# Windowed attention with split fp32r values: no padded key blocks, residual read back in four transfers

## What is computed

```python
# 16 query heads, 4 key/value heads, head width 64, blocks of 128 tokens, window 128
kb, vb = bands(k), bands(v)            # for each block: previous, own and next block; zeros past the ends
scores = einsum('bnqhgd,bnkhd->bnhgqk', qb, kb) * 64 ** -0.5
scores = where(mask, scores, -1e30)    # |distance| <= 128 and inside the sequence
m = maximum(max(scores), sink)
p = exp(scores - m)
probs = p / (sum(p) + exp(sink - m))
out = einsum('bnhgqk,bnkhd->bnqhgd', probs, vb)
...
x = x + concatenate([mixed, mo]) @ w_out[l]          # mo: memory attention
x = x + square(relu(rms_norm(x) @ w_up[l])) @ w_down[l]
```

## Time and profile before

| | |
|---|---|
| median of three runs | 3737.0 us |
| the profiled execution | 3733.89 us, span 3732.1 us, mean granted clock 0.985 |
| busy | PE 3595.5, PEld 2915.6, DVE 1703.1, ACT 969.8, POOL 1058.0 us |
| products L754 | 768 instructions, 101.7 us busy |
| transposes L745 | 384 instructions |
| residual transfers `X<-xT`, 4096 KB | 14.8 us from issue to landing |

### The profile page before, as it was taken

The page is one execution under the profiler, slowest core; times in us unless marked ns, Lnnn a source line. Parts: engine busy times, 40 slices in busy tenths (PEclk is TensorE's granted clock), DMA queues, the critical chain, the costliest instruction groups (busy, mean ns, idle before and its releaser), DMA issues. The chain is left out here.

```text
span 3732.1 us, 44787 instructions
## 1 busy us (share of the span) xinstructions
PE 3595.5 (96%) x16646; PEld 2915.6 (78%) x16646; DVE 1703.1 (46%) x1928; ACT 969.8 (26%) x1556; POOL 1058.0 (28%) x592
## 2 busy tenths in 40 slices
PE   7999999999999999997899999999999999999999
PEld 6867777888888887766788888888688888867877
DVE  7325552444333346884254333334634444453354
ACT  3325552210101013663121011012333242302001
POOL 0110122333323231011333333333244353322350
PEclk9999999999999999998999999999999999999999
DMA  5000001211111112110121111111211111111332
GB/s 188 33 29 12 18 12 68 73 45 51 45 51 45 50 51 104 42 45 18 76 71 46 50 51 45 51 45 51 86 57 45 51 56 40 59 44 45 102 124 79
DMA packets 56423, 210.16 MB, mean 56 GB/s; under 512 B 6000, under 2 KB 10352, under 8 KB 55424
## 3 DMA queue, kind: packets, MB, share of 16 engines
q1 hardware_dynamic: 46352, 158.35, 12.6%
q10 hardware_dynamic: 9968, 50.43, 3.6%
HBM read 186.74 MB, written 22.02 MB: 56 GB/s over the span
## 5 line engine op out<-in xcount | busy, mean ns | idle before, releaser
L486 PE MATMUL G<-Hhi,whi 128*128 128x512 f32 x2528 | 1020.3, 404 | 26.6 <-DVE Hlo L1904 5.5
L486 PE MATMUL G<-Hlo,whi 128*128 128x512 f32 x2528 | 991.2, 392 | 0.0
L486 PE MATMUL G<-Hhi,wlo 128*128 128x512 f32 x2528 | 991.1, 392 | 0.0
L373 POOL CAST whi<-wraw 128x1024 fp32r<-128x1024 f32 (+1 forms) x255 | 264.4, 1037 | 2443.5 <-PE G L486 1125.5
L375 POOL TENSOR_TENSOR wlo<-wraw,whi 128x1024 fp32r<-128x1024 f32 (+1 forms) x255 | 623.8, 2446 | 20.4
L486 PEld LDWEIGHTS G<-Hhi,whi 128*128 128x128 f32 x2528 | 479.5, 190 | 139.3 <-issue 22.6
L486 PEld LDWEIGHTS G<-Hlo,whi 128*128 128x128 f32 x2528 | 479.5, 190 | 104.8 <-issue 7.0
L486 PEld LDWEIGHTS G<-Hhi,wlo 128*128 128x128 f32 x2528 | 478.7, 189 | 101.5
L486 PE MATMUL G<-Ulo,whi 128*128 128x512 f32 x1024 | 398.4, 389 | 0.0
L486 PE MATMUL G<-Uhi,whi 128*128 128x512 f32 x1024 | 398.4, 389 | 0.0
L486 PE MATMUL G<-Uhi,wlo 128*128 128x512 f32 x1024 | 398.4, 389 | 0.0
(11 more groups left out here) (354 smaller groups left out, 4820.9 us busy)
## 6 DMA issues: line engine op xcount, KB each, us to landing
wraw<-wjobs SPq DMA_DIRECT2D x292, 512.0 KB, 3.2
X<-xT ACTq DMA_DIRECT2D x2, 4096.0 KB, 14.8
scratch<-X ACTq DMA_DIRECT2D x2, 4096.0 KB, 14.2
gate_tiles<-gate_st ACTq DMA_DIRECT2D x16, 512.0 KB, 2.8
T<-gate_tiles ACTq DMA_DIRECT2D x16, 512.0 KB, 3.7
X<-scratch ACTq DMA_DIRECT2D x1, 4096.0 KB, 12.8
X<-scratch SPq DMA_DIRECT2D x4, 1024.0 KB, 11.4
out<-yn ACTq DMA_DIRECT2D x8, 512.0 KB, 2.6
```

What stands on the lines that cost most here:

```text
L373: pool.tensor_copy(whi[:, par, 0:kt], wraw[:, par, 0:kt]).then_inc(w_hi, 1)
L486: mm = pe.matmul(G[:, par, cols], w[:, par, k, :], x[:, k, cols], start=(k == 0 and j == 0), stop=(k == kt - 1 and j == 2))
```

## The change

- Keys and values have no padding; a unit in the first or last block has two key blocks (`width`, `key_blocks`), in the scores, mask, exponential, transposes and products. The mask is one table instead of three.
- The values are kept as `vals_hi` and `vals_lo` (fp32r); ScalarE's copy writes `turned_hi`, and a new VectorE operation `low(v)` writes `turned_lo` from PSUM. Three fp32r products of 64 columns replace one plain fp32 product. `turn` of the next unit and `weigh` wait for `low` (`turned_done`) instead of the copy.
- The residual comes back in four transfers of two tiles: 0 and 1 as soon as their place is free, 2 and 3 after the first two and three output jobs; `mo` and others move to make room.
- The last quarter of the first output job is moved behind three quarters of the second; tiles 6 and 7 of `mixed` are split earlier (6 in the last pair, both in layer 1's memory attention); GpSimd splits the second job's weights after the mixed tiles and waits for the last rotation before them.
- Semaphores of the MLP are shared by both layers.

```diff
 mixed = sb("mixed", [P, KT, S], F32, U_AT + 32 * KB)
-mo = sb("mo", [P, MEM_HEADS, S], F32, X_AT)
+mo = sb("mo", [P, MEM_HEADS, S], F32, X_AT + 16 * KB)
 MOhi = sb("MOhi", [P, MEM_HEADS, S], F32R, U_AT)
...
-keys = sb("keys", [P, KV, S + 2 * P], F32, U_AT)
-vals = sb("vals", [P, NBLK + 2, KV * HD], F32, U_AT + 20 * KB)
-cos = sb("cos", [P, S], F32, X_AT + 16 * KB)
-sin = sb("sin", [P, S], F32, X_AT + 20 * KB)
-wmask = sb("wmask", [P, 3, 3 * P], F32, X_AT + 24 * KB)
-probs = sb("probs", [P, 2, 3 * P], F32, X_AT + 29 * KB)
+keys = sb("keys", [P, KV, S], F32, U_AT)
+vals_hi = sb("vals_hi", [P, NBLK, KV * HD], F32R, U_AT + 16 * KB)
+vals_lo = sb("vals_lo", [P, NBLK, KV * HD], F32R, U_AT + 24 * KB)
+cos = sb("cos", [P, S], F32, X_AT)
+sin = sb("sin", [P, S], F32, X_AT + 4 * KB)
+probs = sb("probs", [P, 2, 3 * P], F32, X_AT + 8 * KB)
+turned_hi = sb("turned_hi", [P, 2, 3 * P], F32R, R_AT + 20 * KB + 832)
+turned_lo = sb("turned_lo", [P, 2, 3 * P], F32R, X_AT + 11 * KB)
+wmask = sb("wmask", [P, 3 * P], F32, X_AT + 14 * KB)
...
+def width(v):
+
+    return (2 if v % 16 // 2 in (0, NBLK - 1) else 3) * P
+
 def scored(par, u, width):
...
     splits(MEM_JOBS + 2, START["k"])
-
-    pool.wait_ge(kv_saved, 32)
-    pool.memset(keys[:, :, 0:P], 0.0)
-    pool.memset(keys[:, :, S + P:S + 2 * P], 0.0)
-    pool.memset(vals[:, 0, :], 0.0)
-    pool.memset(vals[:, NBLK + 1, :], 0.0).then_inc(pads, 1)
-    splits(START["k"], START["wo_mixed0"] + 2)
+    splits(START["k"], START["wo_mixed0"])
+    split(START["wo_mixed0"], START["wo_mixed0"] // 2, 0, True)
...
     pool.wait_ge(job_done, START["wo_mixed0"])
+    pool.wait_ge(rot_ok, 2 + 2 * KT)
     for k in range(EARLY):
         split_mixed(0, k, attns["aw"]["oc"], (k + 1) * NBLK)
+    split(START["wo_mixed0"] + 1, START["wo_mixed0"] // 2, 1, True)
     splits(START["wo_mixed0"] + 2, START["wo_mem0"])
...
                 pe.wait_ge(rot_ok, 2 + 2 * p + u // 8 + 1)
-            pe.matmul(scored(p % 2, v, 3 * P), Q[p % 2][:, u % 2, b * P:(b + 1) * P], keys[:, p // 2, b * P:(b + 3) * P],
-                      start=True, stop=True).then_inc(s["sc"], 1)
+            k0, k1 = key_blocks(v)
+            pe.matmul(scored(p % 2, v, (k1 - k0) * P), Q[p % 2][:, u % 2, b * P:(b + 1) * P],
+                      keys[:, p // 2, k0 * P:k1 * P], start=True, stop=True).then_inc(s["sc"], 1)
...
             if v:
-                pe.wait_ge(s["pc"], v)
-            for t in range(3):
+                pe.wait_ge(turned_done, v)
+            k0, k1 = key_blocks(v)
+            for t in range(k1 - k0):
                 tr = pe.transpose(AUX[:, 2, t * P:(t + 1) * P], probs[:, v % 2, t * P:(t + 1) * P], ident)
...
         def weigh(v):
-            p, b, h = v // 16, v % 16 // 2, v % 2
-            pe.wait_ge(s["pc"], v + 1)
+            p, h = v // 16, v % 2
+            pe.wait_ge(turned_done, v + 1)
             if h == 0 and v:
                 pe.wait_ge(s["os"], v // 2)
-            for t in range(3):
-                mm = pe.matmul(AUX[:, 3, h * HD:(h + 1) * HD], probsT[:, v % 2, t * P:(t + 1) * P],
-                               vals[:, b + t, p // 2 * HD:(p // 2 + 1) * HD], start=(t == 0), stop=(t == 2))
+            k0, k1 = key_blocks(v)
+            for t in range(k1 - k0):
+                for j, (w, x) in enumerate(((turned_hi, vals_hi), (turned_hi, vals_lo), (turned_lo, vals_hi))):
+                    mm = pe.matmul(AUX[:, 3, h * HD:(h + 1) * HD], w[:, v % 2, t * P:(t + 1) * P],
+                                   x[:, k0 + t, p // 2 * HD:(p // 2 + 1) * HD], start=(t == 0 and j == 0),
+                                   stop=(k0 + t == k1 - 1 and j == 2))
             mm.then_inc(s["pv"], 1)
...
-        for q in range(12, 16):
-            job_part(q, START[name], 0, Hhi, Hlo, ready)
+
         psum_waits(name, 1, 1)
         pe.wait_ge(*((attns["am"]["oc"], 2 * MEM_HEADS * NBLK) if l else (attns["aw"]["oc"], KT * NBLK)))
-        job(START[name] + 1, 1, Hhi, Hlo, ready)
+        for q in range(12):
+            job_part(q, START[name] + 1, 1, Hhi, Hlo, ready)
+        for j in range(2):
+            for q in range(12, 16):
+                job_part(q, START[name] + j, j, Hhi, Hlo, ready)
         with pe.Fori(1, 4) as i:
...
-            act.wait_ge(l_y, 2 + 7)
+            act.wait_ge(l_y, 2 + 8)
+            for i in range(2):
+                residual_back(1, i)
...
                 query_raw(h + 1, u // 7)
+            elif l and h + 1 == MEM_HEADS and u in (3, 5):
+                act.wait_ge(job_done, START["wo_mixed1"])
+                mixed_high(1, EARLY + u // 5)
         result(U - 2)
...
             act.activation(stat[:, 12 + t:13 + t], vcol("sinks", v // 16 * 2 + v % 2), ACT.Exp, bias=negm)
-            act.activation(probs[:, v % 2, :], probs[:, v % 2, :], ACT.Exp, bias=negm, scale=SINK_SCALE,
-                           accum_out=stat[:, 8 + t:9 + t]).then_inc(s["pr"], 1)
+            e = probs[:, v % 2, 0:width(v)]
+            act.activation(e, e, ACT.Exp, bias=negm, scale=SINK_SCALE, accum_out=stat[:, 8 + t:9 + t])\
+               .then_inc(s["pr"], 1)
...
                 act.wait_ge(s["pv"], v - 1)
-            act.copy(probsT[:, v % 2, :], AUX[:, 2, 0:3 * P]).then_inc(s["pc"], 1)
+            act.copy(turned_hi[:, v % 2, 0:width(v)], AUX[:, 2, 0:width(v)]).then_inc(s["pc"], 1)
...
                 query_raw(p + 1, u // 12)
+            elif p + 1 == KT and u == 4:
+
+                act.wait_ge(rot_ok, 2 + 2 * KT)
+                residual_back(0, 0)
+            elif p + 1 == KT and u == 6:
+                mixed_high(0, EARLY)
         result(U // 2 - 1)
+
+    def residual_back(l, i):
+        tiles = slice(2 * i, 2 * i + 2)
+        act.dma_start(X[:, tiles, :], (xT if l == 0 else scratch[0])[:, tiles, :]).then_inc(x_back[i], 16)
+
+    def mixed_high(l, k):
+        act.copy(Hhi[:, k, :], mixed[:, k, :]).then_inc(split_hi[l], 1)
...
             act.wait_ge(attns["aw"]["oc"], KT * NBLK)
+            mixed_high(0, KT - 1)
+            residual_back(0, 1)
         act.wait_ge(attns["am"]["oc"], (l + 1) * MEM_HEADS * NBLK)
-        for k in range(EARLY, KT):
-            act.copy(Hhi[:, k, :], mixed[:, k, :]).then_inc(split_hi[l], 1)
         for k in range(MEM_HEADS):
...
         act.wait_ge(split_lo[l], KT - EARLY + MEM_HEADS)
-        act.dma_start(X[:], xT if l == 0 else scratch[0]).then_inc(x_back[l], 16)
+        for i in (2, 3):
+            act.wait_ge(job_done, START[f"wo_mixed{l}"] + i)
+            residual_back(l, i)
...
             dve.wait_ge(vt, n + 1)
-            dve.tensor_copy(vals[:, 1:NBLK + 1, n * P:(n + 1) * P], psum.rearrange("p a (b n) -> p (a b) n", n=P))\
-               .then_inc(vcopied, 1)
+            at, v = slice(n * P, (n + 1) * P), psum.rearrange("p a (b n) -> p (a b) n", n=P)
+            dve.tensor_copy(vals_hi[:, :, at], v).then_inc(vsplit, 1)
+            dve.wait_ge(vsplit, n + 1)
+            dve.tensor_tensor(vals_lo[:, :, at], v, vals_hi[:, :, at], ALU.subtract).then_inc(vcopied, 1)
...
             wait_apart(dve, s["sc"], v + 1)
-            m = {0: 0, NBLK - 1: 2}.get(b, 1)
-            chain.link(dve.tensor_tensor_reduce(probs[:, v % 2, :], scored(p % 2, v, 3 * P), wmask[:, m, :],
+
+            mask = wmask[:, P:] if b == 0 else wmask[:, 0:width(v)]
+            chain.link(dve.tensor_tensor_reduce(probs[:, v % 2, 0:width(v)], scored(p % 2, v, width(v)), mask,
                                                 1.0, -3e38, ALU.add, ALU.max, mx))
...
+        def low(v):
+
+            if v >= 2:
+                dve.wait_ge(s["pv"], v - 1)
+            dve.wait_ge(s["pc"], v + 1)
+            w = width(v)
+            dve.tensor_tensor(turned_lo[:, v % 2, 0:w], AUX[:, 2, 0:w], turned_hi[:, v % 2, 0:w], ALU.subtract)\
+               .then_inc(turned_done, 1)
+
         peak(0)
...
                 peak(v + 2)
+            low(v)
             if v and v % 2 == 0:
...
                 heads(p, 1)
+            elif u == 7 and p + 1 == KT:
+                mixed_low(0, EARLY)
         scale_out(U // 2 - 1)
...
-    def add_to_x(name):
-        with dve.Fori(0, 4) as i:
-            for par in range(2):
-                m = i * 2 + par
-                dve.wait_ge(job_done, i * 2 + (START[name] + par + 1))
-                xm = X[:, bass.ds(m, 1), :].rearrange("p a n -> p (a n)")
-                dve.tensor_tensor(xm, G[:, par, :], xm, ALU.add).then_inc(evac["dve"], 1)
+    def mixed_low(l, k):
+        dve.wait_ge(split_hi[l], k - EARLY + 1)
+        dve.tensor_tensor(Hlo[:, k, :], mixed[:, k, :], Hhi[:, k, :], ALU.subtract).then_inc(split_lo[l], 1)
     def project_out(l):
-        for k in range(EARLY, KT):
-            dve.wait_ge(split_hi[l], k - EARLY + 1)
-            dve.tensor_tensor(Hlo[:, k, :], mixed[:, k, :], Hhi[:, k, :], ALU.subtract).then_inc(split_lo[l], 1)
+        if l == 0:
+            mixed_low(0, KT - 1)
         for k in range(MEM_HEADS):
...
```

(45 more changed lines are left out.)

2 lines of the change are left out of this document (1 added, 1 removed).

## The result

The changed kernel takes 3787.41 us (median of 4 runs, 3785.88 to 3789.85), the one before 3735.98 on the same chip: ratio 1.0139, 95% interval 1.0121 to 1.0156. That is +51.4 us where I forecast +14, and outside my range. The profiled execution took 3789.85 us.

What follows compares the result with a forecast made beforehand. TensorE, busy 96% of the span, was taken to bound the kernel. Terms 32.3-10.3+15.6+0.6+0.7-11.6-11.7-2+0.2 = +13.8 took the profiled 3733.9 us to 3747.7; with the runs' median 3.1 higher, the forecast was 3750, range 3740 to 3762.

Steps and rivals of the forecast that it cites:

- Products: Windowed attention: nine passes instead of six at 0.112 us each in 96 units of three key blocks, +32.3 us.
- rivals 2 and 3: Window's products: weight loads don't bind, passes 0.055 apart, 3710 (chance 0.10); wide products' pace holds, 3870 (chance 0.04).
- VectorE's subtraction: Windowed attention: the new step makes TensorE wait 2.2 us a pair, seven pairs, +15.6 us.
- the three places: Waits in each pair: units 12 to 13, units 7 to 11 with rotation and head masks, seam of units 14 to 18.
- Rival 1: Windowed attention: VectorE's new step stays hidden and the last pair gains its 5 us: 3730, chance 0.24.
- Last pair: End of the window: seam gets cheaper, but GpSimd's later splits hold VectorE; lost 10 us against 9.3, +0.7 us.
- Layer 0's projection: Start of its output projection: waits for tile splits and residual go, with slow clock behind them, -11.6 us.
- rival 4: Starts of the output projections: the clock still falls there, +6 us and more, 3757, chance 0.06.
- Layer 1: Start of its output projection: less waiting and slow clock, -11.7 us; memory attention before it, -2 us.
- Units 12 to 13: 0.6 of waiting: Windowed attention, each pair: TensorE waits 0.6 us for VectorE's chain there, 0.26 before.
- Clock 1.00: Sign in the profile after: full clock at the output projections' first jobs and after the second.
- Rival 5: Output projections: a residual tile or split still arrives late, both projections' gains go, 3773, chance 0.05.

Runs made afterwards that it cites:

- e8: The kernel before with the padded units at the window's edges computed over two key blocks instead of three, plain fp32: 3725.72 us, ratio 0.9971.
- e2: The changed kernel with plain fp32 products, without the split of probabilities and values or VectorE's subtraction: 3696.35 us, 0.9897 of the time before.
- e6: e1 without VectorE's subtraction, waits put on ScalarE's copy, the third product reading the high half again: 3730.15 us.
- e1: The changed kernel with one GpSimd query weight split per pair queued behind the scaling it used to hold: 3750.51 us, ratio 1.0040.
- e5: e1 with two products per key block instead of three, VectorE's subtraction still made: 3730.63 us.
- e13: e2 with one transfer of the whole residual per layer at the late place, order of output jobs new: 3710.88 us.
- e10: e2 with the first two output jobs in the order of the kernel before, in both layers: 3694.12 us, 0.9889 of the time before.
- e9: e2 with the residual's four transfers all issued late, behind the last splits of the output projection, in both layers: 3697.23 us.
- e14: e2 with both the four late residual transfers and the old order of the first two output jobs: 3705.98 us (runs 3697.05 to 3708.4).
- e3: The kernel before with two extra one-column VectorE instructions ahead of the two-element add in unit 12 of pairs 0 to 5: 3759.93 us, ratio 1.0063.
- e7: The changed kernel with VectorE's two-element add written as two one-column instructions, GpSimd untouched: 3761.25 us.
- e12: e2 with GpSimd splitting layer 0's mixed tiles right after the last query job, the second output job's weights ahead of them: 3702.79 us.

## Why the prediction was wrong

The total, from the runs: padding -9.8 (e8); what stands around the window -29.4 (e2 less e8); the third product +33.8 (e6 less e2); VectorE's step +20.4 (e1 less e6); the held add and its clock +36.9 (changed kernel less e1). The sum is +51.9; measured +51.4. These are steps of one chain from kernel to kernel, so that they add up proves nothing, and the share of a step depends on the order: along e5 the product is +19.9 and VectorE's step +34.3.

- *Products:* pace and loads right, rivals 2 and 3 out. By my terms products and padding are +22.0; measured -9.8+33.8 = +24.0 along this chain.
- *VectorE's subtraction:* 2.2 us a pair forecast (the three places in fact add up to 2.3), 2.2 measured, at these places. Rival 1 (it stays hidden) is out. What e1 has beyond seven times 2.2 against e6 lies in the last pair, 3.6 longer, and in the first, 5.6 longer: its slow stretch at the window's start lasts 13.7 us in e1 and 6.8 in e6.
- *Last pair:* forecast 44.2 us, 48.4 measured (47.1 in e1).
- *Layer 0's projection:* from the last products to the third job 19.8 us, before 25.4, forecast 16.6. The residual was the right cause (e13), but I left two things out: GpSimd's weight split for the third job starts only when the first job is done, and now has 2.7 us of cover for 3.5; and the clock is still at half for 3.4 us at the start (rival 4, in layer 0 only). The new order, to which I gave the gain, isn't needed for it (e10): the four parts are.
- *Layer 1:* 14.9 us from the first output product to the third job, forecast 13.6, before 20.2. In the attention ahead of it the waits for GpSimd's splits of mixed fell from 3.10 and 0.96 us to 1.96 and 0.99, so -1.1, forecast -2.
- *What brings the 29.4:* the transfers 14.5, GpSimd's later splits 6.4, by difference 8.5 for tile 6's split ahead of the window's end and layer 1's attention, which was not tried alone. Each was undone with the others in place, and e9, e10 and e14 show that such parts stand in for each other, so the 8.5 is a remainder and no measurement. I had 25 for all, of which 5.6 was slow clock. In the profiled executions e8 has 24 us at half clock from the window to layer 0's third job and 44 in layer 1 from its attention on, e2 none and 24: up to 22 of the 29.4 is clock.

**The step that failed** is "Units 12 to 13: 0.6 of waiting", in the term for VectorE's new step. I shifted VectorE's instructions by half a microsecond on a timetable with GpSimd missing from it. What the runs showed in its place: in six pairs the add there takes 2.04 us instead of 0.15, TensorE idles 1.9 us for it, the clock falls to half behind it, and hold and clock together cost 36.9 us (the changed kernel less e1). My timetable had 0.34 us more waiting there and neither hold nor clock. "Clock 1.00" rested on the same gap: I counted clock losses only at the idle spells of 2.8 to 4 us that the trace of before has, while an added 2 us behind the edge units is enough here.

Without the hold the sum stood: e1, which only removes it, took 3750.51 us against my 3750. That it met it to 0.5 us is in part luck: against the runs, my cost of products and padding was 2.0 short, that of VectorE's step with the last pair (16.9) 3.5 short, and what stands around the window brought 4.3 more than the 25.1 that I had. Rival 5 came nearest on the time (3773, still 14 off) and names another cause. No case of mine had the new step push an old VectorE instruction behind one of GpSimd's.

## What to carry to other kernels

Where an edit lengthens a chain on VectorE, lay GpSimd's instructions beside it and ask of every later instruction with two SBUF inputs what it now runs into; an instruction that escapes by 10 ns is a warning row. Price a new stall at its length plus the slow clock behind it: here 11 us of holds came to 37. And undo the parts of a bundle alone: all but the split halves brought 39 us, and the split halves took 91.

## What the runs showed of the hardware

- An idle spell of some 2 us behind units with little TensorE work is enough for the granted clock to go to 0.50 (behind six of six holds in the changed kernel, five of six in e3). It then stayed there for 3.4 us in one pair and 17 in the next, with the same instructions (48.8 and 53.6 us).
- VectorE's one-column TENSOR_SCALAR is not held by GpSimd's subtraction (e7: 14 started while one ran, 0.20 to 0.22 us each), the 512-column one is (2.46 us in e12 instead of 0.49), and so is a TENSOR_TENSOR of two elements (1.99 in e3 instead of 0.15). The subtraction that reads one side from PSUM isn't (six started while one ran in the changed kernel, 0.56 us at most).
- Four transfers of 1024 KB from the same late place (e9) cost 13.7 us less over the two layers than one of 4096 KB (e13): the first add needs only the first part.
